# VectorE writes the first rounded tile behind five closing norms, from products that GpSimd makes, and TensorE multiplies six unread 512 column blocks there

## The chip, the cores and the metric

One Trainium2 chip; the program runs on one of its cores. The metric is device time in microseconds (us), here the median of three runs. Engines: TensorE (PE), VectorE (DVE), ScalarE (ACT), GpSimd (POOL), and SyncE (SP), which issues the transfers of the weights.

## The reference

Two models run one after the other on one sequence of 256 positions and 1024 channels, all in fp32. The first is two layers with attention, a gated linear attention, a recurrent block and convolutional feed forward parts, with a final norm. The second, where the change lies, is two layers of this form:

```python
for l in range(2):
    h = swiglu(rms_norm(x, ffn1_pre[l]), ffn1_w_gate_up[l], ffn1_w_down[l])
    x = x + 0.5 * rms_norm(h, ffn1_post[l])          # closing norm "postA"
    h = hybrid_mixer(rms_norm(x, mix_pre[l]), ...)
    x = x + rms_norm(h, mix_post[l])                 # closing norm "postM"
    h = swiglu(rms_norm(x, ffn2_pre[l]), ffn2_w_gate_up[l], ffn2_w_down[l])
    x = x + 0.5 * rms_norm(h, ffn2_post[l])          # closing norm "postB"
```

`rms_norm(x, g)` is `x / sqrt(mean(x*x) + 1e-6) * g`, the mean over the 1024 channels.

## The kernel before, in words

Activations lie transposed: channels on the 128 partitions, the 256 positions along the free dimension, so the residual `x` is eight tiles of 128x256 (`KT` = 8). An fp32 operand is multiplied as two rounded parts. `xs` (`x_split`) and `hs` (`h_split`) hold for each tile a rounded part (index 0) and the rest (index 1). Weights stream from HBM in chunks of 1 MB (16 blocks of 128x128) into three buffers `w_raw`; ScalarE rounds each into `w_hi` (L224, `round_chunk`), VectorE subtracts to get `w_lo` (L233, `rest_chunk`), both in a ring of four. A product is three matmuls: hi by hi, hi by rest, rest by hi. TensorE waits for `lo_ready` before each chunk. `refill_hi(c)` rounds the chunk four after `c`, `refill_lo(c)` makes the rest of the one three after `c`. So the rest of the third chunk of a stage is made by VectorE's `refill_lo` for the last chunk of the stage before.

Each of the three parts of a layer ends in an output stage (`downA`, `w_o`, `downB`): four groups of two output tiles, evicted by VectorE to scratch (`HB`), squared by ScalarE, the squares added up. The last group is worked tile by tile (`tile_by_tile`, L585 to L588), and behind it TensorE spreads the mean over all partitions with a matrix of 1/1024 (`mean_of`, L360). Then comes the closing norm, five times: `postA` and `postM` in both layers and `postB` in the first. (The second layer's `postB` is the end of the kernel and is written otherwise.)

The norm is folded. The residual is kept divided, and multiplied by the root `RMS` of the new norm: ScalarE takes the root (L365, `root_act`); VectorE (`post_dve`) multiplies `x` by `RMS` (L476) and adds the output tile times its gain (L480), for tiles 0 and 1 singly, then in pairs for the multiply; ScalarE rounds each tile times the gain of the next norm into `xs` (L408, `split_hi`). After the eight tiles VectorE makes the eight rests (L413, `split_lo`), adds up the squares that ScalarE takes (L458; L489, L387, L493), and then makes the rest part of a weight chunk (L233). GpSimd divides `x` by the root later, in the next stage (L381, `residual_pool`).

The next stage begins in `pre_pe`: `alternating` multiplies its first two chunks together, tile by tile as the rounded tiles come (L291), and then by the rests (L298, 32 matmuls); then comes the third chunk in the ordinary way (L251 to L253), with the mean of the next norm behind its first tile (L347). The order on every engine is written out by hand, with semaphores between engines; `tr[...]`, `nxt[...]` are their counters.

Of the kernel before, what the change touches and what calls it, by code (L numbers as in the profile page):

```python
# [26 lines left out]
P = 128  # L27
T = 256
D = 1024
KT = D // P  # L30
# [7 lines left out]
LAYERS2 = 2  # L38
LEVELS = 8
NARROW = 3  # L40
WIDE = ("upA", "upB")


# [51 lines left out]
PRE, ACC, GEL, HID, HB = 0, 8, 16, 20, 24  # L95

YA, PIN, GA, GP, PRE2, ACC2, UU, INV = 0, 8, 16, 24, 32, 38, 41, 44
WIN, DIFF = 16, 20

XC, GB, RR, II, TMP = 0, 8, 16, 24, 32  # L100

# [63 lines left out]
def program(nc, x_in, stream, par1_in, par2_in, ev_const, mask_const, mats, inv_in, out):  # L165
    with ExitStack() as ctx:
# [3 lines left out]
        def sem(name):  # L170
            return ctx.enter_context(nc.semaphore(name))
# [26 lines left out]
        def S(a, n=1):  # L198
            return scr[:, a:a + n, :]

        def S1(a):
            return scr[:, a, :]
# [33 lines left out]
        def refill_lo(dve, c):  # L236

            rest_chunk(dve, c.number + RING - 1)
# [82 lines left out]
        def taken(event):  # L321
            return pair_taken, event + BANKS + 1
# [35 lines left out]
        def mean_of(pe, squares, opens, closes):  # L358

            return pe.matmul(MEAN, ONES, squares, start=opens, stop=closes)  # L360
# [11 lines left out]
        def residual_pool(pool, tr, l, gain=None):  # L372

            pool.wait_ge(*tr["unrms"].count(1, l))
            if gain is not None:
                for k in range(KT):
                    pool.tensor_scalar(x[:, k, :], x[:, k, :], gain[:, k:k + 1], None, ALU.mult)\
                        .then_inc(*tr["scaled"].one())
                pool.wait_ge(*tr["scaled"].count(KT))
            for g in range(KT // 2):  # L380
                pool.tensor_tensor(x[:, 2 * g:2 * g + 2, :], x[:, 2 * g:2 * g + 2, :],  # L381
                                   UNRMS.unsqueeze(1).to_broadcast([P, 2, T]), ALU.mult).then_inc(*tr["resid"].one())
# [61 lines left out]
        def post_tracks(name, layered=True):  # L444
            n = 1 if layered else 0
            return dict(stat=Relay(sem(name + "_stat"), ["mean", "rms"]),
                        y=Signal(sem(name + "_y_ready"), 5 * n), x=Signal(sem(name + "_x_ready"), 8 * n),
                        sq=Signal(sem(name + "_squared"), 4 * n), acc=Signal(sem(name + "_summed"), 5 * n),
                        unrms=Signal(sem(name + "_unrms"), n), resid=Signal(sem(name + "_resid"), 4 * n),
                        scaled=Signal(sem(name + "_scaled")))  # L450
# [4 lines left out]

        def squares_act(act, tr, l):
            for g in range(KT // 2):
                act.activation(S(HB + 2 * g, 2), x[:, 2 * g:2 * g + 2, :], ACT.Square)\  # L458
                   .then_inc(*tr["sq"].one())

        def post_act(act, tr, nxt, gain, l, last):
            root_act(act, tr, l)
            for k in range(KT):
                act.wait_ge(*tr["x"].count(k + 1, l))
                split_hi(act, nxt, gain, k)
            squares_act(act, tr, l)
            refill_hi(act, last)

        def post_dve(dve, tr, gain, nxt, ngain, l, next_layer, last, resid):


            dve.wait_ge(*resid)
            dve.wait_ge(*tr["stat"].after("rms", l))
            for at, ks in enumerate(((0,), (1,), (2, 3), (4, 5), (6, 7))):
                k, n = ks[0], len(ks)
                dve.tensor_tensor(x[:, k:k + n, :], x[:, k:k + n, :], RMS.unsqueeze(1).to_broadcast([P, n, T]),  # L476
                                  ALU.mult).then_inc(*tr["y"].one())
                dve.wait_ge(*tr["y"].count(at + 1, l))
                for j in ks:
                    dve.scalar_tensor_tensor(out=x[:, j, :], in0=S1(HB + j), scalar=gain[:, j:j + 1],  # L480
                                             in1=x[:, j, :], op0=ALU.mult, op1=ALU.add).then_inc(*tr["x"].one())
            for k in range(KT):
                split_lo(dve, nxt, ngain, k, next_layer)
            for g in range(1, KT // 2):
                dve.wait_ge(*tr["sq"].count(g + 1, l))
                if g > 1:
                    dve.wait_ge(*tr["acc"].count(g - 1, l))
                first = S(HB, 2) if g == 1 else sqacc[:, :, :]
                dve.tensor_tensor(sqacc[:, :, :], first, S(HB + 2 * g, 2), ALU.add)\  # L489
                   .then_inc(*tr["acc"].one())  # L490
            fold_dve(dve, sqacc, tr["acc"].count(3, l), tr["acc"].one())
            dve.wait_ge(*tr["acc"].count(4, l))
            dve.scalar_tensor_tensor(out=nxt["total"], in0=MEAN, scalar=D * EPS / P, in1=sqacc[:, 0, :],  # L493
                                     op0=ALU.mult, op1=ALU.add).then_inc(*tr["acc"].one())
            refill_lo(dve, last)

        def final_act(act, tr, gain):

# [49 lines left out]
        def groups(phase, per, layer):  # L548

            for g in range(4):  # L550
                cs = [Chunk(phase, g * per + q, layer) for q in range(per)]
                e = E0[phase] + g * (2 if per > 1 else 1) + layer * LAYER_EVENTS
                yield g, cs, e % BANKS, e
# [25 lines left out]
        def tile_by_tile(pe, c, both, src, k0, nk, first, ready, tr, post, l):  # L579

            for m, dst in enumerate(both):
                for k in range(nk):
                    pe.wait_ge(*ready(k0 + k))
                    b = (k * 2 + m) * P
                    pe.matmul(dst, w_hi[:, c.slot, b:b + P], src[:, k0 + k, 0, :],  # L585
                              start=bool(first) and k == 0, stop=False)
                    pe.matmul(dst, w_hi[:, c.slot, b:b + P], src[:, k0 + k, 1, :], start=False, stop=False)  # L587
                    done = pe.matmul(dst, w_lo[:, c.slot, b:b + P], src[:, k0 + k, 0, :], start=False,  # L588
                                     stop=k == nk - 1)
                done.then_inc(*(tr["tile6_done"].one() if m == 0 else (chunk_done, 1)))  # L590
            if post is not None:
                pe.wait_ge(*tr["acc"].count(4, l))
                if post is PN["last"]:
                    sums_pe(pe, (sqacc[:, 0, :],), True, False)
                    pe.wait_ge(*tr["sq7"].count(1, l))
                    sums_pe(pe, (sqb[:, 1, :],), False, True).then_inc(*post["stat"].one())
                    rinv_pe(pe, post, 0)
                    return
                mean_of(pe, sqacc[:, 0, :], True, False)
                pe.wait_ge(*tr["sq7"].count(1, l))  # L600
                mean_of(pe, sqb[:, 1, :], False, True).then_inc(*post["stat"].one())

        def squares_of(g, nxt):

# [1185 lines left out]
        @block.gpsimd  # L1790
        def _(pool):

            pool.wait_ge(*ev_pe.after("pTc"))
            pool.memset(S(PROB, 12), 0.0).then_inc(decay_zero, 1)
            pool.wait_ge(*ev_dve.after("qs"))
            for t in (1, 0):
                if t == 0:
                    pool.wait_ge(*ev_pe.after("bvT"))
                    pool.wait_ge(apart_ready, 4)
                pool.memset(heads_apart(t), 0.0).then_inc(apart_zero, 1)  # L1800
                pool.wait_ge(apart_zero, 2 - t)
                for h in range(4):
                    if h:
                        pool.wait_ge(apart_ready, 4 * (1 - t) + h)
                    pool.tensor_copy(heads_apart(t)[32 * h:32 * h + 32, h, :], scr[32 * h:32 * h + 32, BQ + t, :])                        .then_inc(apart_ready, 1)
            pool.wait_ge(*ev_dve.after("glo"))
            pool.dma_start(S(INV, 4), inv_in).then_inc(inv_landed, 16)
            up_pool(pool, "up0", FF1, U["up0"], 0)
            up_pool(pool, "up1", FF1, U["up1"], 0)
            pool.wait_ge(inv_landed, 16)  # L1810
            residual_pool(pool, PN["final"], 0, gains("final"))
            for l in range(LAYERS2):
                residual_pool(pool, PN["postA"], l)
                pool_means(pool, l)
                residual_pool(pool, PN["postM"], l)
                if l + 1 < LAYERS2:
                    residual_pool(pool, PN["postB"], l)


# [346 lines left out]
```

## Time and profile before

| | us |
|---|---|
| median of 3 runs | 1906.8 (1906.0 to 1906.86) |
| span of the profiled execution, first to last instruction | 1905.1 |
| TensorE matmuls busy | 1842.2 (97%) |
| VectorE busy | 1448.5 (76%) |
| ScalarE busy | 973.7 (51%) |
| GpSimd busy | 203.4 (11%) |
| DMA | 334.65 MB, mean 176 GB/s |

The profiled execution's own time outside its trace is not given, so its span stands beside the median of the runs; 1.7 us lie between them. Times in rows are us from the span's start. Matmuls are pipelined and their ends are modelled: the distance between the starts of two of them is what TensorE takes for one. The five norms lie near 872, 1094, 1287, 1480 and 1702 us.

### The profile page before, as it was taken

To read this page: it belongs to the slowest core of one execution; us is meant where nothing else is said; L and a number is where in the kernel's file an instruction comes from. 1 tells how busy PE (TensorE), PEld (TensorE's weight loads), DVE (VectorE), ACT (ScalarE), POOL (GpSimd) and SP (SyncE) were. 2 spreads that over 40 slices of the span, in tenths; PEclk is the share of its full clock that TensorE was granted. 3 is DMA by queue.
4 is the path that set the end of the run, shared out by engine and by line. 5 is a ranking of instruction groups with operands and counts; after the bars stand their busy time and mean duration, and the time that the engine had idled before them with its cause. 6 is when DMAs were issued, how large, how long until landed. Compare 5 with 4: busy or idle time off the path is not lost.

```text
span 1905.1 us, 31454 instructions
## 1 busy us (share of the span) xinstructions
PE 1842.2 (97%) x13110; PEld 1728.2 (91%) x13110; DVE 1448.5 (76%) x1728; ACT 973.7 (51%) x1169; POOL 203.4 (11%) x160
## 2 busy tenths in 40 slices
PE   7978999999999999999999999999999999999997
PEld 7958999999999898889999998898889999998887
DVE  6796998578899578757885797759775886579774
ACT  5453765467666455544353455545554445355552
POOL 0020332000233003000500010001000220001000
PEclk9989999999999999999999999999999999999999
DMA  7413555534455545554454435553555345445551
GB/s 287 150 45 120 177 182 197 199 125 166 176 200 179 198 170 184 185 213 161 155 216 178 177 147 194 207 204 133 199 198 216 142 170 203 155 155 199 186 212 67
DMA packets 46789, 334.65 MB, mean 176 GB/s; under 512 B 5185, under 2 KB 5569, under 8 KB 6465
## 3 DMA queue, kind: packets, MB, share of 16 engines
q1 hardware_dynamic: 46512, 332.20, 48.2%
q8 instruction: 104, 1.70, 0.3%
q0 software_dynamic: 144, 0.52, 0.1%
q14 instruction: 29, 0.23, 0.0%
HBM read 331.65 MB, written 1.05 MB: 175 GB/s over the span
## 4 chain that ended last, share of the span: by engine, by line
PE 84%; DVE 9%; ACT 2%; POOL 2%; issue 1%; DMA 1%; SPq 0%; DVEq 0%; ACTq 0%
PE psum L267 25%; PE psum L270 13%; PE psum L251 11%; PE psum L253 11%; PE psum L252 11%; PE psum L291 7%; PE psum L298 3%; DVE w_lo L233 2%; POOL scratch L1636 1%; POOL x_resid L381 1%; PE psum L587 1%; PE psum L585 1%; PE psum L588 1%; POOL scratch L1633 1%; DVE scratch L1670 1%
## 5 line engine op out<-in xcount | busy, mean ns | idle before, releaser
L224 ACT ACTIVATE w_hi<-w_raw 128x2048 fp32r<-128x2048 f32 x313 | 597.6, 1912 | 449.4 <-PE psum L253 185.6
L233 DVE TENSOR_TENSOR w_lo<-w_raw,w_hi 128x2048 fp32r<-128x2048 f32 x313 | 724.6, 2319 | 36.9 <-ACT w_hi L224 36.8
L251 PE MATMUL psum<-x_split,w_hi 128*128 128x256 f32 x1768 | 505.1, 286 | 12.6 <-DVE x_split L413 10.5
L253 PE MATMUL psum<-x_split,w_lo 128*128 128x256 f32 x1768 | 501.2, 283 | 0.0
L252 PE MATMUL psum<-x_split,w_hi 128*128 128x256 f32 x1768 | 501.1, 283 | 0.0
L267 PE MATMUL psum<-x_split,w_hi 128*128 128x512 f32 x1216 | 429.8, 399 | 0.0
L251 PEld LDWEIGHTS psum<-x_split,w_hi 128*128 128x128 f32 x1768 | 340.3, 192 | 15.4 <-issue 14.0
L270 PE MATMUL psum<-x_split,w_lo 128*128 128x256 f32 x1216 | 341.5, 281 | 0.0
L252 PEld LDWEIGHTS psum<-x_split,w_hi 128*128 128x128 f32 x1768 | 340.3, 192 | 0.4
L253 PEld LDWEIGHTS psum<-x_split,w_lo 128*128 128x128 f32 x1768 | 340.2, 192 | 0.0
L267 PE MATMUL psum<-h_split,w_hi 128*128 128x512 f32 x816 | 288.6, 399 | 0.0
L267 PEld LDWEIGHTS psum<-x_split,w_hi 128*128 128x128 f32 x1216 | 228.5, 188 | 56.9
L270 PEld LDWEIGHTS psum<-x_split,w_lo 128*128 128x128 f32 x1216 | 229.7, 189 | 0.0
L270 PE MATMUL psum<-h_split,w_lo 128*128 128x256 f32 x816 | 229.2, 281 | 0.0
L267 PEld LDWEIGHTS psum<-h_split,w_hi 128*128 128x128 f32 x816 | 153.3, 188 | 38.1
L270 PEld LDWEIGHTS psum<-h_split,w_lo 128*128 128x128 f32 x816 | 154.2, 189 | 0.0
L251 PE MATMUL psum<-h_split,w_hi 128*128 128x256 f32 x480 | 139.6, 291 | 5.0 <-ACT scratch L1195 2.5
L381 POOL TENSOR_TENSOR x_resid<-x_resid,squares 128x512 f32<-128x512 f32 x24 | 46.4, 1964 | 913.1 <-DVE squares L370 913.0
L252 PE MATMUL psum<-h_split,w_hi 128*128 128x256 f32 x480 | 138.0, 288 | 0.0
L253 PE MATMUL psum<-h_split,w_lo 128*128 128x256 f32 x480 | 138.0, 287 | 0.0
L318 DVE TENSOR_TENSOR scratch<-psum,inv_rms 128x512 f32<-128x512 f32 (+1 forms) x129 | 87.3, 683 | 64.8 <-PE psum L253 64.5
L758 ACT ACTIVATE scratch<-psum 128x512 f32<-128x512 f32 x76 | 45.5, 598 | 175.5 <-PE psum L270 175.3
(238 smaller groups left out, 2447.8 us busy)
## 6 DMA issues: line engine op xcount, KB each, us to landing
w_raw<-stream_in SPq DMA_DIRECT2D x313, 1024.0 KB, 4.8
x_resid<-x_in SPq DMA_DIRECT2D x1, 1024.0 KB, 7.0
y_out<-x_resid SPq DMA_DIRECT2D x4, 256.0 KB, 2.5
scratch<-mask_in SPq DMA_DIRECT2D x1, 768.0 KB, 10.9
scratch<-ev_in SPq DMA_DIRECT2D x1, 512.0 KB, 9.5
scratch<-inv_in POOLq DMA_DIRECT2D x1, 512.0 KB, 4.3
params<-par_in SPq DMA_DIRECT2D x1, 247.0 KB, 7.2
matrices<-mat_in SPq DMA_DIRECT2D x1, 192.0 KB, 8.8
```

The costliest lines, as they stand in the source:

```text
L224: act.activation(w_hi[:, n % RING, :], raw[:, n % RAWS, :], ACT.Copy).then_inc(hi_ready, 1)
L233: dve.tensor_tensor(w_lo[:, n % RING, :], raw[:, n % RAWS, :], w_hi[:, n % RING, :].bitcast(F32), ALU.subtract).then_inc(lo_ready, 1)
L251: pe.matmul(dst, w_hi[:, c.slot, b:b + P], src[:, k0 + k, 0, :], start=opens, stop=False)
L252: pe.matmul(dst, w_hi[:, c.slot, b:b + P], src[:, k0 + k, 1, :], start=False, stop=False)
L253: done = pe.matmul(dst, w_lo[:, c.slot, b:b + P], src[:, k0 + k, 0, :], start=False, stop=last and k == nk - 1 and m == len(tiles_) - 1)
L267: pe.matmul(ps[:, bank_, :], w_hi[:, c.slot, b:b + P], src[:, k0 + k, :, :].rearrange("p a t -> p (a t)"), start=first and k == 0, stop=False)
L270: done = pe.matmul(tile(bank_, 0), w_lo[:, c.slot, b:b + P], src[:, k0 + k, 0, :], start=False, stop=last and k == nk - 1)
L291: pe.matmul(tile(c.bank, m), w[:, c.slot, b:b + P], src[:, k0 + k, 0, :], start=k == 0 and m == 0 and w is w_hi, stop=False)
L298: done = pe.matmul(tile(c.bank, m), w_hi[:, c.slot, b:b + P], src[:, k0 + k, 1, :], start=False, stop=k == nk - 1 and m == 1)
L318: dve.tensor_tensor(dst, bank(c.bank, tiles), rinv[:, :].unsqueeze(1).to_broadcast([P, tiles, T]), ALU.mult).then_inc(pair_taken, 1)
L381: pool.tensor_tensor(x[:, 2 * g:2 * g + 2, :], x[:, 2 * g:2 * g + 2, :], UNRMS.unsqueeze(1).to_broadcast([P, 2, T]), ALU.mult).then_inc(*t ...
L758: act.activation(S(ACC + 2 * c.slot, 2), ps[:, c.bank:c.bank + 2, T:2 * T], ACT.Copy)\
```

## The change

In the five closing norms:

- GpSimd gets a new function `post_pool`. Before the root is there it makes three products of tile 0: the residual times the next gain (`FIRST_X`), the output tile times both gains (`FIRST_H`), the output tile times its own gain (`FIRST_G`). Behind the root it makes the residual's tile 0: `x * RMS`, and `+ FIRST_G`.
- VectorE makes from the first two products the rounded tile 0 of `xs` itself, with a multiply and an add, in place of its multiply and gain-and-add of `x`'s tile 0. ScalarE no longer rounds tile 0.
- VectorE waits for GpSimd's tile 0 before the eight rests, ScalarE before its first squares.
- TensorE, behind the mean, multiplies six blocks of 512 columns out of `h_split` into PSUM bank 7, which nobody reads.

```diff
+AWAKE = 6
+FIRST_X, FIRST_H, FIRST_G, FIRST_ROOT = 32, 33, 34, 35
...
         def squares_act(act, tr, l):
             for g in range(KT // 2):
+                if g == 0:
+                    act.wait_ge(*tr["first"].count(2, l))
...
-            for k in range(KT):
-                act.wait_ge(*tr["x"].count(k + 1, l))
+            for k in range(1, KT):
+                act.wait_ge(*tr["x"].count(k, l))
                 split_hi(act, nxt, gain, k)
...
             dve.wait_ge(*resid)
             dve.wait_ge(*tr["stat"].after("rms", l))
-            for at, ks in enumerate(((0,), (1,), (2, 3), (4, 5), (6, 7))):
+            dve.wait_ge(*tr["parts"].count(2, l))
+            dve.tensor_tensor(S1(FIRST_ROOT), S1(FIRST_X), RMS, ALU.mult).then_inc(*tr["y"].one())
+            dve.wait_ge(*tr["y"].count(1, l))
+            dve.tensor_tensor(xs[:, 0, 0, :], S1(FIRST_ROOT), S1(FIRST_H), ALU.add).then_inc(*nxt["hi"].one())
+            for at, ks in enumerate(((1,), (2, 3), (4, 5), (6, 7)), 1):
...
+            dve.wait_ge(*tr["first"].count(2, l))
             for k in range(KT):
                 split_lo(dve, nxt, ngain, k, next_layer)
...
+        def post_pool(pool, tr, phase, per, gain, ngain, l, resid):
+            _, _, _, event = next(iter(groups(phase, per, l)))
+            pool.wait_ge(*resid)
+            pool.wait_ge(*taken(event + (1 if per > 1 else 0)))
+            pool.tensor_scalar(S1(FIRST_X), x[:, 0, :], ngain[:, 0:1], None, ALU.mult).then_inc(*tr["parts"].one())
+            pool.tensor_scalar(S1(FIRST_H), S1(HB), gain[:, 0:1], ngain[:, 0:1], ALU.mult, ALU.mult)\
+                .then_inc(*tr["parts"].one())
+            pool.tensor_scalar(S1(FIRST_G), S1(HB), gain[:, 0:1], None, ALU.mult).then_inc(*tr["parts"].one())
+            pool.wait_ge(*tr["parts"].count(3, l))
+            pool.wait_ge(*tr["stat"].after("rms", l))
+            pool.tensor_tensor(x[:, 0, :], x[:, 0, :], RMS, ALU.mult).then_inc(*tr["first"].one())
+            pool.wait_ge(*tr["first"].count(1, l))
+            pool.tensor_tensor(x[:, 0, :], x[:, 0, :], S1(FIRST_G), ALU.add).then_inc(*tr["first"].one())
...
                 mean_of(pe, sqb[:, 1, :], False, True).then_inc(*post["stat"].one())
+                awake_pe(pe, src, AWAKE)
+
+        def awake_pe(pe, src, n):
+            for k in range(n):
+                pe.matmul(ps[:, 7, :], src[:, k, 0, 0:P], src[:, k, :, :].rearrange("p a t -> p (a t)"),
+                          start=True, stop=True)
```

`post_pool` is called on GpSimd ahead of `residual_pool` for `postA` and `postM` in both layers and for `postB` in the first.

## Rows read from the trace of the kernel before

**Rows 1.** The page, chain that ended last: share of the span by engine.
```profile
PE 84%; DVE 9%; ACT 2%; POOL 2%; issue 1%; DMA 1%; SPq 0%; DVEq 0%; ACTq 0%
```

**Rows 2.** TensorE's waits, whole span: us in total, times, longest.
```profile
PE psum L291 <- ACT x_split L408: 11.2, 5, 2.2
...
PE psum L1114 <- DVE scratch L1389: 1.9, 1, 1.9
...
PE psum L251 <- DVE w_lo L233: 1.5, 3, 0.6
```

**Rows 3.** Timeline, first closing norm: start, duration, instruction, idle before and releaser.
```profile
871.94 0.47 ACT L365 ACTIVATE squares<-psum,small 128x256 f32<-128x256 f32 x1 [0.79 <-PE psum L360]
872.52 0.43 DVE L476 TENSOR_TENSOR x_resid<-x_resid,squares 128x256 f32<-128x256 f32 x1 [0.84 <-ACT squares L365]
872.98 0.48 DVE L480 SCALAR_TENSOR_TENSOR x_resid<-scratch,params,x_resid 128x256 f32<-128x256 f32 x1
873.38 0.42 DVE L476 TENSOR_TENSOR x_resid<-x_resid,squares 128x256 f32<-128x256 f32 x1
873.50 0.51 ACT L408 ACTIVATE x_split<-x_resid,params 128x256 fp32r<-128x256 f32 x1 [1.08 <-DVE x_resid L480]
...
874.15 0.36 PE L291 MATMUL psum<-x_split,w_hi 128*128 128x256 f32 x1 [2.25 <-ACT x_split L408]
```

**Rows 4.** Stretches: length, busy time by engine, granted TensorE clock (PEclk), DMA.
```profile
99.00:103.00 4.00, 1.97 (x18) 1.65 (x20) 2.72 (x4) 3.94 (x6) 2.66 (x1) 1.00 0.00 0
...
872.00:875.40 3.40, 1.25 (x10) 1.28 (x11) 2.77 (x7) 1.44 (x3) 0.00 (x0) 1.00 0.00 0
875.42:878.80 3.38, 3.38 (x19) 3.38 (x17) 3.31 (x9) 2.10 (x5) 0.00 (x0) 0.50 0.00 0
```

**Rows 5.** Timeline of TensorE: two neighbours at the lower clock.
```profile
876.03 0.41 PE L291 MATMUL psum<-x_split,w_lo 128*128 128x256 f32 x1
876.24 0.41 PE L291 MATMUL psum<-x_split,w_hi 128*128 128x256 f32 x1
```

**Rows 6.** Timeline of VectorE: the rests and the third chunk's `w_lo`.
```profile
878.79 3.25 DVE L413 SCALAR_TENSOR_TENSOR x_split<-x_resid,params,x_split 128x256 fp32r<-128x256 f32 x8
...
885.07 2.28 DVE L233 TENSOR_TENSOR w_lo<-w_raw,w_hi 128x2048 fp32r<-128x2048 f32 x1
```

**Rows 7.** Timeline of TensorE where the third chunk begins.
```profile
886.73 0.64 PE L298 MATMUL psum<-x_split,w_hi 128*128 128x256 f32 x4
887.50 0.35 PE L251 MATMUL psum<-x_split,w_hi 128*128 128x256 f32 x1
```

**Rows 8.** Chain that ended last, third norm, at the same place: start, us, what.
```profile
1300.00 2.21 DVE w_lo L233
...
1302.35 0.35 PE psum L251
```

**Rows 9.** GpSimd by line: instructions, duration ns min/median/max, first and last start.
```profile
L858 POOL TENSOR_TENSOR scratch<-scratch x48: 913/919/2944, 200.7 to 620.7; 128x256 f32<-128x256 f32 x48
...
L864 POOL TENSOR_TENSOR h_split<-scratch,h_split x48: 731/745/1292, 206.4 to 624.0; 128x256 fp32r<-128x256 f32 x48
...
L381 POOL TENSOR_TENSOR x_resid<-x_resid,squares x24: 1297/1586/3351, 725.1 to 1742.3; 128x512 f32<-128x512 f32 x24
```

**Rows 10.** Timelines of VectorE and GpSimd where both work.
```profile
1125.65 0.42 DVE L792 TENSOR_TENSOR scratch<-scratch 128x256 f32<-128x256 f32 x1
...
1128.14 7.75 POOL L381 TENSOR_TENSOR x_resid<-x_resid,squares 128x512 f32<-128x512 f32 x4 [186.57 <-DVE squares L370]
...
1129.92 3.38 DVE L233 TENSOR_TENSOR w_lo<-w_raw,w_hi 128x2048 fp32r<-128x2048 f32 x1
...
1133.22 1.51 DVE L792 TENSOR_TENSOR scratch<-scratch 128x256 f32<-128x256 f32 x1
...
716.60 0.62 DVE L792 TENSOR_TENSOR scratch<-scratch 128x256 f32<-128x256 f32 x1
```

More of the change, by code:

```diff
@@ L446, in post_tracks @@
             return dict(stat=Relay(sem(name + "_stat"), ["mean", "rms"]),
-                        y=Signal(sem(name + "_y_ready"), 5 * n), x=Signal(sem(name + "_x_ready"), 8 * n),
+                        y=Signal(sem(name + "_y_ready"), 5 * n), x=Signal(sem(name + "_x_ready"), 7 * n),
+                        parts=Signal(sem(name + "_first_tile_parts"), 3 * n),
+                        first=Signal(sem(name + "_first_tile_done"), 2 * n),
                         sq=Signal(sem(name + "_squared"), 4 * n), acc=Signal(sem(name + "_summed"), 5 * n),
@@ L1812, in _ @@
             for l in range(LAYERS2):
+                post_pool(pool, PN["postA"], "downA", 3, gains2("postA", l), gains2("mpre", l), l,
+                          resid_before("postA", l))
                 residual_pool(pool, PN["postA"], l)
                 pool_means(pool, l)
+                post_pool(pool, PN["postM"], "w_o", 1, gains2("mpost", l), gains2("preB", l), l,
+                          resid_before("postM", l))
                 residual_pool(pool, PN["postM"], l)
                 if l + 1 < LAYERS2:
+                    post_pool(pool, PN["postB"], "downB", 3, gains2("postB", l), gains2("nextA", l), l,
+                              resid_before("postB", l))
                     residual_pool(pool, PN["postB"], l)
```

## The prediction, made before the changed kernel ran

> **What bounds the kernel now.** I read the page's chain by engine first: 84% of the span is a chain through TensorE and 9% one through VectorE [rows 1]. So the edit matters only where TensorE is not fed. TensorE's waits name the place: five waits of 2.2 us, one in each closing norm that the edit touches, for ScalarE's first rounded tile `x_split`, 11.2 us in all [rows 2]. That is the sum that the edit seems to aim at. In the timeline of the first norm the reader is to see how such a wait comes about: root 871.94 to 872.41, VectorE's multiply at 872.52, its gain-and-add at 872.98, ScalarE's rounding 873.50 to 874.01, and the first product at 874.15 [rows 3]. Then comes the clock. It is granted at 1.00 until 875.40 and at 0.50 (1.2 GHz, not 2.4) from 875.42 to 878.80, after TensorE had stood 2.25 us [rows 4]. The products then start 0.21 apart [rows 5], not 0.12 (four of 0.28 each within 0.64, so 0.36 over three distances) [rows 7]: sixteen of them take 3.4 us and would take 1.9, so a lapse is 1.5 us of TensorE's time. All five norms have it.
>
> The sum of both, 2.1 us a norm, would be the gain if TensorE's own time decided when the norm is over. It does not. The third chunk of the stage behind the norm needs its rest part `w_lo`, and VectorE makes that last, behind the residual, the eight rests of `x_split` and the sums. In the first norm VectorE is busy with these from 878.79 on, starts that `w_lo` at 885.07 and ends it at 887.35 [rows 6]; TensorE starts the chunk at 887.50, 0.15 later, and some 0.3 after its products of the two chunks before it (four from 886.73, 0.12 apart) would have let it [rows 7]. The distance from the start of that `w_lo` to the chunk's first product is 2.42 or 2.43 us in all five norms; in the third, where the clock lapsed earliest, the chain of waits itself runs through `w_lo` into it [rows 8]. So the norm's end is set by VectorE's chain, 15.56 us from the root's start (871.94) to that product (887.50). Both losses of TensorE lie inside it, beside work that takes as long.
>
> **The change part by part.**
>
> *First tile, VectorE.* Removed: a multiply and a gain-and-add, 872.52 to the next multiply at 873.38, 0.86 us [rows 3]. Added: the multiply into `FIRST_ROOT` and an add into `x_split`, both 128x256 `TENSOR_TENSOR` with two operands in SBUF. The multiply again takes 0.46 with its wait, the add 0.34 before the next can start (0.42 less the overlap of 0.08 that the rows of such instructions have): 0.80. Gain 0.06 us a norm; the wait for `parts`, met long before, is counted as nothing. ScalarE's first rounding (0.51) goes from the way to tile 0, but ScalarE's other tiles follow VectorE as before, and VectorE does not wait for tile 0's rounding until far later. Gain on the norm's end: none of its own.
>
> *First tile, GpSimd.* Its three products by gains come long before, when the first output pair is out. Beside one such pass (the gains of the final norm, near 716) VectorE's 128x256 multiply took 0.62 against 0.42 [rows 10]. At worst that is 3 x 0.20 in a stage in which VectorE waits on TensorE: taken as nothing; if VectorE's slack before the mean were gone, up to 0.6 in the two `postM` norms, 1.2 together, kept for the upper end.
>
> The two passes behind the root (`x * RMS`, `+ FIRST_G`) are the ones that count. They are released by the same event as VectorE's chain and run in its first 2 us. The trace shows what this costs: while GpSimd did four 128x512 residual multiplies from 1128.14 (1.30 each where undisturbed) [rows 9, 10], VectorE's 128x256 multiply took 1.51 against 0.42 shortly before, and a `w_lo` 3.38 against 2.28 [rows 6]. Each pass thus put 1.09 to 1.10 on a VectorE instruction with two SBUF operands, 0.21 less than its own length. All instructions of the new chain are of that kind. GpSimd's 128x256 passes take 0.745 (subtract) or 0.919 (multiply) [rows 9], so one costs VectorE 0.54 to 0.71: I take 0.62, two of them 1.24. Lower bound: 0.20 each, the milder row, 0.40. Upper: the full length, 2 x 0.92 = 1.84. Whichever engine goes first, the first pass holds up the multiply or the add, and the second the instruction after it.
>
> On the blocking length the Trainium skill is harsher: "SBUF — State Buffer", on the shared port pair, says that against a GpSimd instruction that reads SBUF a VectorE instruction with two SBUF inputs fully blocks until the first to issue has finished. By that the two passes would cost their whole 1.5 to 1.8 us a norm, and the five norms 7.1 to 8.9 in all rather than the 5.9 below; the rows show 0.21 less per pass.
>
> *Sum for the chain.* 1.24 - 0.06 = 1.18 us a norm, 5.9 us over five; bounds 5 x 0.34 = 1.7 and 5 x 1.78 = 8.9. After the third chunk TensorE is the bound again, so the shift goes to the end of the kernel in full. The new wait of VectorE for GpSimd's tile 0 (`first`) stands before the eight rests, near 880; GpSimd should be done by 875.5. Behind it would queue those rests, the sums and the `w_lo`. Cost: none. `squares_act` waits for the same and begins at 879: none.
>
> *Six 512 column blocks.* They run at 0.21 each at full clock (double the 0.12 of a half as wide product, rounded down for the fixed part), 1.3 us, from about 871.9 to 873.2. The first tile is written at 873.3 without GpSimd's passes and at 873.9 to 874.6 with one or both in front, so the blocks delay nothing. TensorE now idles about 1.2 us there instead of 2.25, and the clock may hold. That gives TensorE up to 1.5 us which it can't spend: starting at 874.4, with 96 products of 0.12 and about 0.9 of waiting for tiles 1 and 2, it is through at 886.8 and then waits for a `w_lo` that ends at 887.35 + 1.18 = 888.5. A wait of 0.2 to 0.3 becomes one of about 1.9 us, right before the stretch where TensorE is the bound. If the clock lapses behind that wait, 1.5 us are lost for good; the lapses of today cost nothing, being hidden by VectorE's chain. Each of the five waits of 2.25 was followed by a lapse; one wait of 1.9 us in the attention was not, the clock stayed at 1.00 [rows 2, 4]. I take a chance of one in four to a third per norm, a lapse in one of five: 1.5 us; bounds 0 and 7.5. Where the clock lapses early in spite of the blocks, TensorE comes to the third chunk just in time, as now, and nothing is lost.
>
> Total: 5.9 + 1.5 = +7.4 us. The span of the profiled execution is 1905.1, the median of the runs 1906.8; the 1.7 between them is kept: 1906.8 + 7.4 = 1914.2.
>
> **The rivals.**
>
> *R1, TensorE gains (faster).* The first tile comes 0.65 sooner and the clock holds: up to 2.1 us a norm, 10.7 in all, 1896; with the first tile alone 3.3, 1903.5. For it: the 11.2 us of waits and the five lapses. Against it: the third chunk's `w_lo`. TensorE's side decides from the point where that `w_lo` ends before TensorE is through the first two chunks: 887.35 today against 885.5 or so with the clock held. Short of that the norm gains what VectorE's chain loses, and nothing in the edit shortens that by more than 0.06. Chance 0.04.
>
> *R2, VectorE is not held up, no lapse.* GpSimd's passes slip into VectorE's holes: 5 x (-0.06) = -0.3, 1906.5. Against it: the rows with 1.51. Chance 0.11.
>
> *R3, not held up, but lapses behind the longer wait in three to five norms.* 4.5 to 7.5 less 0.3: 1911 to 1914. The wait is then about 2.0, nearer to the 2.25 that always had one. Chance 0.10.
>
> *R4, held up, and lapses in three to five norms.* 5.9 + 4.5 to 7.5: 1917.2 to 1920.2. Chance 0.15.
>
> *R5, the edit does not do what it says:* GpSimd's tile 0 is late and VectorE waits for it before the rests. It would take passes stretched to 3 us each, as when one stands behind a `w_lo`; none runs there. 1 to 2 us a norm on top, 1920 and more. Chance 0.02.
>
> **How the numbers follow.** Forecast (held up by the port, a lapse in none to two norms): chance 0.58, its own range 1909.5 to 1917. About 0.2% (3.8 us) is what a measurement of this kernel can tell from no change. Faster: R1, 0.04. Same: R2, 0.11. Slower: forecast 0.58, R3 0.10, R4 0.15, R5 0.02, together 0.85. The range leaves out R1, R2 and the far end of R4 and R5: 1908.5 to 1919.
>
> **What would show it.** (1) From the root's start to the third chunk's first product 16.7 us instead of 15.56. (2) VectorE's first add, first multiply or tile 1's multiply at about 1.0 instead of 0.42, twice a norm, beside GpSimd's two passes. (3) TensorE's wait before its first `x_split` product down to 1.0 to 1.5. (4) TensorE's wait for `w_lo` before the third chunk up from about 0.3 to 1.5 to 2 where the clock held. (5) Clock 0.50 in fewer or other stretches; a lapse behind the third chunk's start is a loss, one before it is not. I am wrong if VectorE's chain keeps its 0.42 durations (R2, R3), or if the third chunk starts sooner than 15.3 us after the root (R1).

## The result, and the profile after

The changed kernel takes 1911.05 us (median of 18 runs, 1909.96 to 1911.64), the kernel before 1906.57 beside it (18 runs). The ratio is 1.0021, 95% interval 1.0015 to 1.0027: slower by 4.0 us by the ratio (2.9 to 5.1), 4.5 by the medians. Forecast were 7.4 slower, with a range of 1908.5 to 1919. The span of the profiled execution is 1909.8, 4.7 over that of before.

The page of the changed kernel, chain that ended last; TensorE has lost 4 points of it, VectorE won 4 [rows 1]:

```profile
PE 80%; DVE 13%; POOL 2%; ACT 2%; issue 1%; DMA 1%; SPq 0%; DVEq 0%; ACTq 0%
```

TensorE's waits over the whole span, as in [rows 2]:

```profile
PE psum L253 <- DVE w_lo L235: 9.2, 7, 1.6
...
PE psum L293 <- ACT x_split L410: 4.2, 6, 1.0
PE psum L293 <- DVE x_split L483: 3.3, 5, 0.7
```

The edit did to TensorE what it says. The 11.2 us before the first tile of `x_split` are down to 3.3, with 4.2 before later tiles. But the wait for `w_lo` grew from 1.5 to 9.2: what TensorE saved stands there, and with it the time by which `w_lo` itself now comes later. The first closing norm, VectorE, GpSimd and ScalarE, against [rows 3] (start, duration, instruction):

```profile
872.26 0.47 ACT L367 ACTIVATE squares<-psum,small 128x256 f32<-128x256 f32 x1 [0.79 <-PE psum L362]
...
872.82 0.42 DVE L481 TENSOR_TENSOR scratch<-scratch,squares 128x256 f32<-128x256 f32 x1 [0.83 <-ACT squares L367]
873.28 0.84 DVE L483 TENSOR_TENSOR x_split<-scratch 128x256 fp32r<-128x256 f32 x1
874.04 0.94 DVE L486 TENSOR_TENSOR x_resid<-x_resid,squares 128x256 f32<-128x256 f32 x1
875.02 0.48 DVE L490 SCALAR_TENSOR_TENSOR x_resid<-scratch,params,x_resid 128x256 f32<-128x256 f32 x1
875.42 0.68 DVE L486 TENSOR_TENSOR x_resid<-x_resid,squares 128x512 f32<-128x512 f32 x1
...
872.88 0.96 POOL L519 TENSOR_TENSOR x_resid<-x_resid,squares 128x256 f32<-128x256 f32 x1 [40.75 <-ACT squares L367]
873.91 0.79 POOL L521 TENSOR_TENSOR x_resid<-x_resid,scratch 128x256 f32<-128x256 f32 x1
```

The reader is to see two VectorE instructions of 0.84 and 0.94 that take 0.42 elsewhere, each beside one pass of GpSimd. VectorE's first 128x512 multiply starts 3.16 after the root's start (875.42 - 872.26). Before, that was 2.30 (874.24 - 871.94), so two instructions account for the whole 0.86:

```profile
874.24 0.69 DVE L476 TENSOR_TENSOR x_resid<-x_resid,squares 128x512 f32<-128x512 f32 x1
```

TensorE's timeline in the same norm, against [rows 3, 7]:

```profile
871.87 1.74 PE L633 MATMUL psum<-h_split 128*128 128x512 f32 x6
874.26 0.36 PE L293 MATMUL psum<-x_split,w_hi 128*128 128x256 f32 x1 [0.66 <-DVE x_split L483]
...
876.10 0.39 PE L293 MATMUL psum<-x_split,w_hi 128*128 128x256 f32 x1 [0.66 <-ACT x_split L410]
...
888.68 0.35 PE L253 MATMUL psum<-x_split,w_hi 128*128 128x256 f32 x1 [1.60 <-DVE w_lo L235]
```

The same stretch in one row, as in [rows 4]: the third number from the end is the granted clock.

```profile
874.00:889.00 15.00, 12.47 (x99) 12.02 (x100) 14.58 (x27) 7.13 (x12) 0.70 (x1) 1.00 0.01 2
```

The first product starts 2.00 after the root's start, 0.2 sooner than before (2.21). The clock is held at 1.00, in this norm and in the other four. None of this gain reaches the end of the norm: the third chunk starts 16.42 after the root's start (888.68 - 872.26), before it was 15.56. In all five norms it is 16.42, and 15.55 or 15.56 before: 0.87 us a norm, 4.35 over five, against the 4.0 to 4.5 that were timed.

### The profile page after: what moved, and what is told of

It reads as the page before. It is cut to its first block, busy times and chain, and to the rows that moved or that the text cites. A ratio compares the mean times of both kernels' runs of the same rounds, so it can differ in the third digit from the quotient of the medians.

```text
span 1909.8 us, 31549 instructions
## 1 busy us (share of the span) xinstructions
PE 1842.3 (96%) x13140; PEld 1724.1 (90%) x13140; DVE 1453.3 (76%) x1728; ACT 971.4 (51%) x1164; POOL 244.7 (13%) x185
## 4 chain that ended last, share of the span: by engine, by line
PE 80%; DVE 13%; POOL 2%; ACT 2%; issue 1%; DMA 1%; SPq 0%; DVEq 0%; ACTq 0%
PE psum L269 25%; PE psum L272 13%; PE psum L253 11%; PE psum L255 11%; PE psum L254 11%; PE psum L293 4%; DVE w_lo L235 3%; PE psum L300 2%; DVE x_split L415 1%; POOL scratch L1669 1%; POOL x_resid L383 1%; DMA w_raw<-stream_in 1%; DVE x_resid L490 1%; DVE x_resid L486 1%; POOL scratch L1666 1%
## 5 line engine op out<-in xcount | busy, mean ns | idle before, releaser
L841 DVE SCALAR_TENSOR_TENSOR scratch<-scratch,params 128x255 f32<-128x255 f32 x192 | 120.5, 687 | 3.6 <-ACT scratch L783 2.8
```

The source lines that it names most:

```text
L841: dve.scalar_tensor_tensor(out=scr[:, ACC + 2 * s + t, d:T], in0=scr[:, PRE + 2 * s + t, 0:T - d], scalar=conv[0][:, bass.ds(((c.n - prev) ...
```

## The experiments

Two theories. **Chain:** VectorE's work from the root to the third chunk's `w_lo` sets the norm's end; GpSimd's two passes behind the root lengthen it; TensorE's waits and its lapsed clock lie beside it. **TensorE:** the time of the first product and the clock count, and the loss comes from something else (waits, products, blocks). Four kernels take the change apart, five move the `w_lo` out of the way, one asks what in a GpSimd pass it is that counts. Each median is of 5 to 18 runs. "Third chunk" is the distance from the root's start to that chunk's first product in the five norms of the profiled execution. "Clock lapsed" is the number of norms in which the granted clock fell to 0.50 behind the mean.

| kernel | median us | ratio to before (95%) | third chunk, us | clock lapsed |
|---|---|---|---|---|
| before | 1906.57 | | 15.55 to 15.56 | 5 of 5 |
| changed | 1911.05 | 1.0021 (1.0015 to 1.0027) | 16.42 | 0 |
| no_passes | 1905.95 | 0.9994 (0.9985 to 1.0003) | 15.47 to 15.49 | 0 |
| passes_only | 1911.29 | 1.0025 (1.0015 to 1.0035) | 16.34 to 16.35 | 5 |
| blocks_only | 1906.37 | 0.9998 (0.9989 to 1.0007) | 15.55 to 15.56 | 0 |
| no_blocks | 1912.28 | 1.0030 (1.0018 to 1.0042) | 16.41 to 16.43 | 3 |
| early_rest | 1903.61 | 0.9981 (0.9972 to 0.9990) | 15.28, 13.80, 15.29, 13.79, 15.30 | 3 |
| early_rest_blocks | 1898.53 | 0.9955 (0.9942 to 0.9969) | 13.79 to 13.81 | 0 |
| after_early_rest | 1903.09 | 0.9980 (0.9971 to 0.9989) | 14.66 to 14.67 | 0 |
| early_rest_ceiling | 1899.52 | 0.9960 (0.9946 to 0.9973) | 13.71 to 13.73 | 0 |
| writes_only | 1906.81 | 1.0000 (0.9991 to 1.0010) | 15.55 to 15.57 | 4 |
| early_rest_3_blocks | 1899.72 | 0.9964 (0.9951 to 0.9978) | 13.79 to 13.80 | 0 |

The kernel before stood at 1906.87 beside the first four, 1906.96 beside the next four and 1907.04 beside the last two.

**no_passes.** The changed kernel without GpSimd's two passes behind the root. VectorE's wait for them goes too, and ScalarE waits for the early products instead; tile 0 of the residual is left without its update.

```diff
-            pool.wait_ge(*tr["stat"].after("rms", l))
-            pool.tensor_tensor(x[:, 0, :], x[:, 0, :], RMS, ALU.mult).then_inc(*tr["first"].one())
-            pool.wait_ge(*tr["first"].count(1, l))
-            pool.tensor_tensor(x[:, 0, :], x[:, 0, :], S1(FIRST_G), ALU.add).then_inc(*tr["first"].one())
```

> The changed kernel without GpSimd's two passes behind the root (x * RMS and + FIRST_G); tile 0 of the residual is left undivided by them, so its values are left out of what is computed. The three early products, VectorE's own rounded tile 0 and the six blocks stay. Port theory (the passes hold VectorE up by 0.94 us a norm): VectorE's chain is then 0.06 us a norm shorter than in the kernel before, root to third chunk 15.49 us instead of 16.42, and the time is 1906.3, 0.3 under the kernel before and 4.5 to 5 under the changed one. Rival (the extra products, waits or the six blocks cost the time): it stays at 1909 to 1911.

VectorE's timeline in the first norm of this kernel:

```profile
871.68 0.42 DVE L481 TENSOR_TENSOR scratch<-scratch,squares 128x256 f32<-128x256 f32 x1 [0.83 <-ACT squares L367]
872.14 0.42 DVE L483 TENSOR_TENSOR x_split<-scratch 128x256 fp32r<-128x256 f32 x1
872.49 0.42 DVE L486 TENSOR_TENSOR x_resid<-x_resid,squares 128x256 f32<-128x256 f32 x1
```

Both instructions are back at 0.42, the new pair takes 0.81 instead of 0.86, and the loss is gone: 1905.95, third chunk at 15.48. The first product now starts 1.60 after the root, 0.6 sooner than before, the clock is held, and all that is worth 0.07 us a norm.

**passes_only.** The kernel before with two passes that read the root and write scratch that no other engine uses. ScalarE also waits for them before its first squares, as in the changed kernel; writes_only below has the same wait and loses nothing.

```diff
+            pool.wait_ge(*tr["stat"].after("rms", l))
+            pool.tensor_tensor(S1(32), RMS, RMS, ALU.mult).then_inc(*tr["first"].one())
+            pool.wait_ge(*tr["first"].count(1, l))
+            pool.tensor_tensor(S1(33), S1(32), RMS, ALU.add).then_inc(*tr["first"].one())
```

> The kernel before with two GpSimd passes of 128x256 behind the root, on scratch tiles that nobody uses, and nothing else of the change. Port theory: two of VectorE's first instructions after the root are longer by 0.4 to 0.6 each, the distance from root to third chunk grows from 15.55 to about 16.45, the time is 1906.6 + 4.5 = 1911.1. The clock lapses as in the kernel before, hidden. Rival (only passes that share data with VectorE's chain delay it, through the waits): no change, 1906.6.

Timelines of VectorE and GpSimd in its first norm:

```profile
872.17 0.87 DVE L479 TENSOR_TENSOR x_resid<-x_resid,squares 128x256 f32<-128x256 f32 x1 [0.84 <-ACT squares L365]
873.08 0.83 DVE L483 SCALAR_TENSOR_TENSOR x_resid<-scratch,params,x_resid 128x256 f32<-128x256 f32 x1
873.83 0.41 DVE L479 TENSOR_TENSOR x_resid<-x_resid,squares 128x256 f32<-128x256 f32 x1
...
872.15 0.61 POOL L503 TENSOR_TENSOR scratch<-squares 128x256 f32<-128x256 f32 x1 [139.53 <-ACT squares L365]
872.84 0.79 POOL L505 TENSOR_TENSOR scratch<-scratch,squares 128x256 f32<-128x256 f32 x1
```

The whole loss, without any other part of the change: third chunk 16.34, 1911.29. The passes need not write anything that VectorE uses; they share with it only the reading of the root. Together with no_passes this settles where the loss comes from.

**blocks_only.** The kernel before with `awake_pe(pe, src, AWAKE)` behind the mean, `AWAKE = 6`.

```diff
                 mean_of(pe, sqb[:, 1, :], False, True).then_inc(*post["stat"].one())
+                awake_pe(pe, src, AWAKE)
```

> The kernel before with the six blocks of 512 columns behind the mean and nothing else. Theory (VectorE's chain to the third chunk's w_lo sets the end of the norm): the clock no longer lapses, TensorE waits some 1.8 us before the third chunk instead of 0.3, the distance root to third chunk stays 15.55 and the time 1906.6 within 0.5. Rival (TensorE's time counts): each lapse was worth 1.5 us, 1899. Second rival (the longer wait brings the clock down behind the third chunk): up to 1.5 us a norm more, 1908 to 1914.

Where its third chunk begins, TensorE's timeline:

```profile
887.10 0.36 PE L252 MATMUL psum<-x_split,w_hi 128*128 128x256 f32 x1 [1.61 <-DVE w_lo L234]
```

No lapse in five norms, so TensorE has 1.5 us a norm more, and stands for it before the third chunk. Time and third chunk are those of before. The fear that this longer wait brings the clock down behind the third chunk's start is not borne out: 0 of 5 here, 0 of 5 in the changed kernel.

**no_blocks.** The changed kernel with `AWAKE = 0`.

> The changed kernel with no blocks (AWAKE = 0). Theory: TensorE idles about 2.0 us behind the mean, the clock lapses there again in most norms, hidden behind VectorE's chain; root to third chunk stays 16.42 and the time is 1910.9, that of the changed kernel. Rival (the blocks save 1.5 us a norm): 1918.

Third chunk at 16.42 as expected, whether the clock lapsed or not. The median is 1912.28 and its interval overlaps that of the changed kernel; its third chunks give no ground for a difference. Two of the five waits behind the mean (2.0 us each) were not followed by a lapse: the clock over the first norm and over the second, by stretches:

```profile
873.30:876.00 2.70, 2.06 (x15) 1.85 (x16) 2.63 (x6) 0.85 (x2) 0.40 (x1) 1.00 0.00 0
1097.30:1100.30 3.00, 2.35 (x12) 2.22 (x11) 2.93 (x7) 1.56 (x4) 0.00 (x0) 0.56 0.00 0
```

**early_rest.** The kernel before, with the `w_lo` that gates the third chunk ahead of the sums, and the next mean three tiles later in that chunk.

```diff
                 split_lo(dve, nxt, ngain, k, next_layer)
+            refill_lo(dve, last)
             for g in range(1, KT // 2):
...
-            refill_lo(dve, last)
...
-                    whole(pe, c, hooks={0: lambda: mean_pe(pe, tr, summed, l), 2: mean})
+                    whole(pe, c, hooks={(3 if ph != "up0" and tr in (N["normA"], N["normM"], N["normB"]) and mean is NONE else 0): lambda: mean_pe(pe, tr, summed, l), 2: mean})
```

(The condition is true behind the five closing norms, where the place is 3, and false elsewhere, where it stays 0.)

> The kernel before with VectorE's w_lo for the third chunk made right behind the eight rests of x_split, ahead of the sums of squares, and the mean of the next norm taken three tiles later in that chunk, so that it need not wait for the sums; no blocks, no first tile. Theory (that w_lo gates the third chunk, the lapsed clock is hidden just beside it): w_lo is ready about 3 us sooner, but TensorE with its lapse arrives only 0.3 sooner: root to third chunk 15.26, 5 x 0.3 = 1.5 less, 1905.2. Rival (w_lo is not what the third chunk waits for): 15.55 and 1906.7.

Its timelines: `w_lo` in the first norm, then root and third chunk of the first norm and of the second:

```profile
882.38 2.29 DVE L233 TENSOR_TENSOR w_lo<-w_raw,w_hi 128x2048 fp32r<-128x2048 f32 x1
...
872.36 0.47 ACT L365 ACTIVATE squares<-psum,small 128x256 f32<-128x256 f32 x1 [0.79 <-PE psum L360]
887.64 0.28 PE L251 MATMUL psum<-x_split,w_hi 128*128 128x256 f32 x1
...
1093.90 0.47 ACT L365 ACTIVATE squares<-psum,small 128x256 f32<-128x256 f32 x1 [1.36 <-PE psum L360]
1107.70 0.28 PE L251 MATMUL psum<-x_split,w_hi 128*128 128x256 f32 x1
```

`w_lo` is ready at 884.67, 3 us before TensorE wants it. Now the clock shows in the end of the norm: 15.28 where it lapsed, 13.80 where it did not, 1.49 apart. In two norms the same wait of 2.2 us was not followed by a lapse. I had expected five lapses; with three the gain at the third chunks is 3 x 0.27 + 2 x 1.76 = 4.3 instead of 1.5, and 3.4 were measured by the medians. (The lapses are counted in one execution of the eleven, which ran from 1901.5 to 1905.5; how many the others had is not known.)

**early_rest_blocks.** Both edits: the early `w_lo` and the six blocks.

> The same with the six blocks behind the mean. Theory: with w_lo out of the way TensorE's own time sets the norm, and the lapse of the clock counts at last. In the kernel with the blocks alone TensorE would have been ready 13.79 us after the root: 1.76 a norm less than 15.55, 8.8 in all, 1898. Rival (the blocks save no time that TensorE can use): like the kernel with the early rest alone, 1905. Second rival (the sums, now late, hold up the mean and the evictions, and give the gain back): 1903 or more, with waits of VectorE or TensorE near the third to fifth chunk.

Its third chunk in the first norm (root at 871.08), and VectorE there:

```profile
884.88 0.28 PE L252 MATMUL psum<-x_split,w_hi 128*128 128x256 f32 x1
...
881.10 2.29 DVE L234 TENSOR_TENSOR w_lo<-w_raw,w_hi 128x2048 fp32r<-128x2048 f32 x1
883.30 0.69 DVE L493 TENSOR_TENSOR square_sum<-scratch 128x512 f32<-128x512 f32 x1
884.09 1.49 DVE L493 TENSOR_TENSOR square_sum<-square_sum,scratch 128x512 f32<-128x512 f32 x2
```

1898.53, the fastest median of all: 8.4 us under the kernel before by the medians, against 8.8 expected. The blocks that were worth nothing alone are worth 5.1 on top of the early rest (1903.61 - 1898.53). The sums end at 886.5 and the mean is taken at 887.8, so TensorE does not wait for the sums.

The second rival is true in part all the same. TensorE's waits, whole span:

```profile
PE psum L268 <- DVE scratch L319: 0.8, 3, 0.3
```

The mean now comes 16.68 us after the root instead of 16.34, and VectorE's first eviction of the next stage, which needs it, 19.67 instead of 19.33. In the stages behind the second, third and fifth norm TensorE wants that eviction's bank before it is free and stands 0.28. From root to root these stages are shorter by 1.28 and 1.29 (and 1.24 from the last root to the end), those behind the first and the fourth by 1.78 and 1.75. So the profile shows 7.3 of the 8.8 behind the first root. Of the 8.2 by which its span is shorter, 0.9 lie ahead of the first root, where nothing was edited; that the timed 8.4 comes so near to 8.8 is in part luck.

**after_early_rest.** The changed kernel with the same two moves.

> The changed kernel with the same early w_lo and later mean. Theory: TensorE sets the norm here too, but its tiles come 0.87 later because GpSimd's passes delay VectorE; it would have been ready 14.66 after the root: 0.9 a norm under the kernel before, 4.5 in all, 1902.2, and some 4 slower than the same without the first tile. Rival (GpSimd's delay is now hidden, and the first tile 0.2 earlier counts): equal to or under the kernel with early rest and blocks, 1898 or less.

1903.09, third chunk at 14.67. With `w_lo` out of the way the first tile with its GpSimd passes still costs 0.87 a norm, since the passes delay the tiles that TensorE waits for: 4.6 us slower than early_rest_blocks. The passes alone cost 0.95 (against early_rest_ceiling, which follows).

**early_rest_ceiling.** The same without GpSimd's two passes: what the first tile would be worth at no cost.

> The changed kernel with the early w_lo and later mean, and without GpSimd's two passes behind the root, so tile 0 of the residual is not brought up to date. It shows the most that the early first tile could be worth if it cost nothing. Theory: tiles 1 and 2 still come from ScalarE no sooner than before, so the 0.6 us by which the first product is earlier become waits before the products of tiles 1 and 2; TensorE is ready 13.72 instead of 13.79 after the root: 0.07 a norm, 1897.6, not to be told from the kernel with early rest and blocks. Rival (the first product's time is what counts): 0.6 a norm, 3 less, 1895.

Third chunk 13.72, 0.08 us under early_rest_blocks; the time is 1899.52 and their intervals overlap. So VectorE's first tile is worth nothing that the times show, even free of charge and with TensorE as the bound.

**writes_only.** As passes_only, with two instructions that only write.

```diff
-            pool.tensor_tensor(S1(32), RMS, RMS, ALU.mult).then_inc(*tr["first"].one())
+            pool.memset(S(32, 3), 0.0).then_inc(*tr["first"].one())
...
-            pool.tensor_tensor(S1(33), S1(32), RMS, ALU.add).then_inc(*tr["first"].one())
+            pool.memset(S(32, 3), 0.0).then_inc(*tr["first"].one())
```

> The kernel before with two GpSimd instructions of about the same length behind the root that only write: memsets of 128x768 on scratch that nobody uses. If it is GpSimd's reading that holds VectorE's two-operand instructions up, root to third chunk stays 15.55 and the time 1906.7. Rival (any work of GpSimd at that moment delays VectorE): about 16.3 and 1911, as with the two reading passes.

Timelines of VectorE and GpSimd in its first norm:

```profile
871.50 0.42 DVE L479 TENSOR_TENSOR x_resid<-x_resid,squares 128x256 f32<-128x256 f32 x1 [0.84 <-ACT squares L365]
871.96 0.48 DVE L483 SCALAR_TENSOR_TENSOR x_resid<-scratch,params,x_resid 128x256 f32<-128x256 f32 x1
...
871.46 0.74 POOL L503 MEMSET scratch<- 128x768 f32 x1 [139.50 <-ACT squares L365]
872.25 0.74 POOL L505 MEMSET scratch<- 128x768 f32 x1
```

VectorE runs at 0.42 and 0.48 beside two GpSimd instructions of 0.74. Two instructions that only write don't hold VectorE up; two that also read do. The Trainium skill says this in "SBUF — State Buffer", section "Who interferes with whom": a VectorE instruction with two SBUF inputs contends with a GpSimd instruction that reads SBUF, not with one that only writes it; passes_only and writes_only agree.

**early_rest_3_blocks.** early_rest_blocks with `AWAKE = 3`.

> The early w_lo with three blocks instead of six. TensorE then stands about 1.6 us behind the mean instead of 1.0 with six and 2.2 with none, where two of five norms had no lapse. If three are enough the third chunk starts 13.8 after the root in all five norms and the time is 1898.5; if not, each norm with a lapse adds 1.5: with two of them 1901.5, with none spared 1904 to 1905.

No lapse in five norms, third chunk at 13.80, 1899.72: the intervals overlap, so three are not to be told from six.

## Why the prediction was right, and where it was off

- *The chain to the third chunk's `w_lo` sets the norm's end.* Shown: the five third chunks move by what VectorE's chain moves and by nothing else as long as that `w_lo` is late (no_passes, blocks_only, passes_only), and follow TensorE's clock as soon as it is early (early_rest).
- *VectorE's own pair of instructions, 0.06 shorter.* Shown: 15.55 to 15.48 in no_passes, 0.07.
- *GpSimd's passes, 1.24 a norm.* Right in kind, too large: 0.42 and 0.52 in the changed kernel, 0.94 together. This is the term that was mis-sized. The price was taken as the length of a pass less 0.21, with lengths of 0.919 and 0.745. What the held instruction pays is what is left of the pass when it starts, less 0.14. In the changed kernel it ends 0.28 after the pass (873.84 to 874.12 and 874.70 to 874.98), as it does in passes_only (872.76 to 873.04 and 873.63 to 873.91), and takes 0.42 alone: 0.56 - 0.14 and 0.66 - 0.14. The rows of [rows 10] obey the same rule. Two of the four passes that stand there in one line, from GpSimd's timeline of the kernel before:

```profile
1129.40 1.75 POOL L381 TENSOR_TENSOR x_resid<-x_resid,squares 128x512 f32<-128x512 f32 x1
1131.10 3.35 POOL L381 TENSOR_TENSOR x_resid<-x_resid,squares 128x512 f32<-128x512 f32 x1
```

  They end at 1131.15 and 1134.45; VectorE's instructions came at 1129.92 and 1133.22, with 1.23 left of each pass, and paid 1.10 and 1.09. The passes are 1.75 and 3.35 long, not 1.30, because they stood themselves, until VectorE's instruction before was through: a recorded pass holds its own wait. So does the 0.919 that was priced. One of these passes of L858 with the VectorE instruction before it, and one of L864 with no VectorE instruction beside it:

```profile
218.60 0.92 POOL L858 TENSOR_TENSOR scratch<-scratch 128x256 f32<-128x256 f32 x1
...
217.95 0.96 DVE L808 SCALAR_TENSOR_TENSOR scratch<-scratch,params 128x255 f32<-128x255 f32 x1
...
206.42 0.73 POOL L864 TENSOR_TENSOR h_split<-scratch,h_split 128x256 fp32r<-128x256 f32 x1
```

  VectorE's instruction runs until 218.91, and 0.61 of the pass come after it. It is so in the changed kernel: the pass of 0.96 begins at 872.88 beside a multiply that ends at 873.24, with 0.60 to come; the one of 0.79 begins at 873.91 beside the add that ends at 874.12, with 0.58 to come. VectorE's next instruction starts at about that point and finds some 0.6 left (0.56 and 0.66); less 0.14 that is an estimate of 0.46 a pass, where 0.62 was taken. With 0.94 the chain comes to 0.88 a norm, 4.4 in all, against 4.35 read and 4.0 to 4.5 timed.
- *The Trainium skill's harsher price, the full pass.* By recorded lengths (1.75 for both) it is too high: 0.94 were paid. But for the first 0.36 and 0.21 of them the VectorE instruction before still ran. Of the 1.18 behind that, 0.94 were paid, so VectorE stood for most of it. The runs contradict the sum of 7.1 to 8.9; that one engine stands while the other's instruction runs, they bear out but for the 0.14.
- *A lapse of the clock behind the longer wait for `w_lo`, 1.5 us in one norm of five.* Did not occur in the profiles: ten waits of 1.60 to 1.61 in the changed kernel and blocks_only, five more in no_passes, and the clock stayed at 1.00 behind all of them. The wait was also shorter than the 1.9 that I had worked out. This term, 1.5 in the forecast, is zero in what the profiles show.
- *The edit's gain on TensorE.* Shown to exist and to be hidden: 11.2 us of waits for the first tile became 3.3, and the lapses went from five to none, for nothing.
- *GpSimd's three early products and the wait for `first`: nothing.* Shown for both together: no_passes keeps the products and is no slower than before; VectorE's rests follow its last residual tile without a hole in the changed kernel (879.97, with the tile until 880.06). What the products alone cost was not measured apart.
- *The signs.* Four came, the first two smaller than written (16.42 and not 16.7; 0.84 and 0.94, not about 1.0). The third was off: TensorE's wait before the first product fell to 0.66, below the 1.0 to 1.5 expected, since the six blocks stand for 1.74 in the row and not for 1.3.

The forecast of 7.4 is 3.0 more than the 4.4 of the chain: 1.5 were the lapse and 1.5 (5 x 0.3) the price of the passes. The measured time lies at the edge of R3 (1911 to 1914, no hold-up but lapses) as well, and nearer to it than to 1914.2; only the durations of VectorE's instructions and the clock tell the two apart. R1 fell: without a way past `w_lo` TensorE's gain is worth nothing. R2 is what no_passes shows, and did not come about. R3 and R4 fell with the lapse, R5 with GpSimd's tile being ready at 874.70.

## What to carry to other kernels

An engine's largest wait is not what a stage costs: before shortening it, find the next thing that this engine waits for. If it stands there already, as here for `w_lo` (0.3 us), nothing of what seems to be on offer (here 2.1 us a norm) will arrive. An engine that is off the path is not free when it reads SBUF beside the engine that is on it. Here the price was what was left of its pass when the other's instruction came, less 0.14 us, and the recorded length of a pass held waits of its own, so a length from a busy stretch can't be taken as work. And an order on the path may hold the whole gain: the kernel before, with one 2.3 us instruction moved ahead of sums that nobody needed yet and six unread products to hold the clock, was 8.4 us faster, where the change made it 4 slower.

## What the runs showed that I had not expected

- A wait of 2.2 us of TensorE behind the mean brought the clock from 2.4 down to 1.2 GHz in five of five norms in the kernel before, but in three of five in early_rest and in four of five in writes_only, where the wait was the same; waits of 2.0 did in three of five in no_blocks. What decides between two equal waits no run shows. A lapse, where it came, cost 1.49 us (15.29 against 13.80). Waits of 1.6 before the third chunk never did, in 18 cases (5 each in the changed kernel, no_passes and blocks_only, 2 in no_blocks, 1 in writes_only).
- Three blocks of 512 columns held the clock as well as six in the five norms of one profile.
- The distance from root to third chunk differs by 0.02 us at most between norms of one kernel with the same clock, so it told 0.07 us a norm, where the medians had intervals of about 0.1% of 1907, some 2 us each way.
